# A gated recurrence interleaved with projection products: spawned twelve weight pieces earlier, at three steps to two pieces instead of four

## The chip, the cores and the metric

One core of a Trainium2 chip runs the whole program. The metric is the device time of one execution in microseconds (us); the table below gives the median of three executions of the kernel before.

## What is computed

The program is two transformer blocks on 256 tokens of width 1024, all in float32. The part that matters here lies near its start. The first block normalizes x, modulates it to h, and multiplies h by one wide matrix `w_in`, whose column groups feed several branches. One branch is a gated linear recurrence (`hgrn2`), eight heads of width 128:

```
f = lb + (1.0 - lb) * jax.nn.sigmoid(f_pre.astype(jnp.float32))
log_f = jnp.log(f)
kk = 1.0 - f
...
attn = jnp.einsum('bhtd,bhsd,bhtsd->bhts', qt, kt, decay)
o = (jnp.einsum('bhts,bhsv->bhtv', attn, vt)
     + jnp.einsum('bhtd,bhdv->bhtv', qt * jnp.exp(b), state))
```

Its inputs are the products bq (q), bf (f) and bi (v) of h with `w_in`. Other products of h (iq, ik, iw, aq, ak, av) feed a sparse attention, which comes after the recurrence in the program.

## The kernel before, in words

**Products by pieces.** Every product runs on TensorE as three fast passes (lines 579, 580, 581) over operands split into a high and a low part. Weights arrive by DMA from the SP queue into five slots, and are cut into pieces of 128x1024. For each piece ScalarE writes the high part (line 1398), VectorE the low part (line 2025), and TensorE then does 24 matmuls of 128x256 or 12 of 128x512. Four slots hold split pieces, so ScalarE and VectorE prepare piece n+3 while TensorE is at piece n; the high part of piece n+3 waits until piece n-1 has been used. When a piece ends a product, ScalarE copies the finished bank out (line 1420, or line 1426 with two copies), which waits for TensorE to end that very piece.

**The pieces in question**, in the order of the program behind the products bf and bq: bi (8 pieces), iq (4), ik (1), iw (1, with small matmuls of 128x8), aq (8), ak (8), av (8). This text numbers them 1 to 38: bi is 1 to 8, iq 9 to 12, ik 13, iw 14, aq 15 to 22, ak 23 to 30, av 31 to 38. Of aq and ak every second piece (16, 18, ... 30) ends a product; of av pieces 34 and 38.

**The recurrence by steps.** On each of the four engines `hgrn()` is a Python generator (TensorE line 709, ScalarE line 1466, VectorE line 2127, GpSimd line 2928) whose `yield`s cut it into 56 steps, 28 for each half of the heads. `Ticks` (line 69) runs it: after each piece `tick()` takes `rate` steps of the generator on that engine, and `join()` takes what is left. So the place of every instruction is set when the program is built, alike on all engines. In each half the steps are these: step 2 and 3 make two score tiles (line 720). Then come eight levels, and level l has its steps at 4+3l, 5+3l and 6+3l:

- step A (4+3l): ScalarE takes two exponentials (lines 1488 and 1494). VectorE multiplies Q (line 2150) and adds to P (line 2155). GpSimd multiplies K (line 2954) and adds to S (line 2957).
- steps T0 and T1 (5+3l and 6+3l): TensorE multiplies K and Q to a tile each (line 732, four matmuls of 128x128), and VectorE copies it by mask (line 2164).

A tile T0 waits for Q of VectorE and K of GpSimd of its level. Q waits for the first exponential and for T1 of the level before, K for the second exponential and for the same T1. Level 7 has one tile; behind it, steps 27 and 28 of a half form the outputs (lines 745, 747 and 748), the first of which waits for ScalarE to copy the tile of level 7 out (line 1501).

**Where it stands.** `ticks.spawn(hgrn(), 2)` stands behind bi and iq (TensorE line 1288). 26 pieces follow with 2 steps each, that is 52 steps; `ticks.join()` behind av takes the last four. The attention begins behind the join, and its first matmul (line 755) waits for two small loads, which the SP queue issues only after the last output of the recurrence (line 745 ff.) is done.

Of the kernel before, what the change touches and what calls it, by code (L numbers as in the profile page):

```python
# [70 lines left out]
class Ticks:  # L71
# [3 lines left out]
        self.gens, self.ended, self.all = [], set(), False  # L75

    def spawn(self, gen, rate=1):
        self.gens.append([gen, rate])

    def tick(self):  # L80
        for b in list(self.gens):
            for _ in range(b[1]):
                if next(b[0], "end") == "end":
                    self.gens.remove(b)
                    break
# [47 lines left out]
def build(nc, a, out, scr):  # L133
    with ExitStack() as ctx:
# [242 lines left out]
        def skey(p, what):  # L377

            return (what, p.j)
# [174 lines left out]
        def tensor(e, w):  # L554
            ticks = Ticks()
# [37 lines left out]
            def gemm1(name, X, ready, at=None):  # L593

                o = {}
                for p in walk(name):
                    if at and (p.g, p.k) in at:
                        enter(*at[p.g, p.k])
                    w.wait_ge(*skey(p, "L"))
                    for i in range(p.m):  # L600
                        k = p.k + i
                        w.wait_ge(*ready(k))
                        for t in range(2):
                            if k == 0:
                                o[t] = take("m", name, p.g, t)
                            rows = slice(128 * t, 128 * t + 128)
                            ins = three(o[t][:, 0:p.width], (X[0][:, k, rows], X[1][:, k, rows]),
                                        parts(p, i * p.width, p.width), k == 0, p.end and i == p.m - 1)
                    used(ins, p, *([(name, p.g, t) for t in range(2)] if p.end else []))
# [99 lines left out]
            def hgrn():  # L709
                for hf in range(2):  # L710
                    q_, k_ = bq[:, 1024 * hf:1024 * hf + 1024], bk[:, 1024 * hf:1024 * hf + 1024]
                    S_, Q_, K_, E_ = hg
                    yield
                    for tile in range(2):
                        w.wait_ge("kk")
                        w.wait_ge("bq", 3)
                        b = take("s", "hgd", hf, tile)
                        for g in range(4):
                            c = slice(256 * g + 128 * tile, 256 * g + 128 * tile + 128)
                            ins = e.matmul(b[:, 128 * g:128 * g + 128], k_[:, c], q_[:, c], start=True, stop=True)  # L720
                        full(ins, "hgd", hf, tile)
                        yield
                    for li in range(8):
                        yield
                        w.wait_ge("hgtQ", hf, li)
                        w.wait_ge("hgtK", hf, li)
                        for tile in range(2 if li < 7 else 1):
                            b = take("s", "hgl", hf, li, tile)
                            for g in range(4):
                                c = slice(256 * g + 128 * tile, 256 * g + 128 * tile + 128)  # L730
                                c2 = c if li < 7 else slice(256 * g + 128, 256 * g + 256)
                                ins = e.matmul(b[:, 128 * g:128 * g + 128], K_[:, c], Q_[:, c2], start=True, stop=True)  # L732
                            full(ins, "hgl", hf, li, tile)
                            yield
                    w.wait_ge("taken", ("hgl", hf, 6, 1))
                    w.wait_ge("taken", ("hgl", hf, 7, 0))
                    for t in range(2):
                        w.wait_ge("bi", 1)
                        b = take("s", "hgo", hf, t)
                        for g in range(4):  # L740
                            h = 4 * hf + g
                            o = b[:, 128 * g:128 * g + 128]
                            v = [bi[:, i * 1024 + h * 128:i * 1024 + h * 128 + 128] for i in range(2)]
                            if t == 0:
                                ins = e.matmul(o, hgA[:, g, 0:128], v[0], start=True, stop=True)
                            else:
                                e.matmul(o, hgA[:, g, 256:384], v[0], start=True, stop=False)
                                ins = e.matmul(o, hgA[:, g, 128:256], v[1], start=False, stop=True)
                        full(ins, "hgo", hf, t)
                        yield  # L750
# [511 lines left out]
            b = take("m", "c")  # L1262
# [8 lines left out]
            b = take("m", "rows", 0)  # L1271
# [8 lines left out]
            b = take("m", "rows", 1)  # L1280
            e.transpose(b[:, 0:128], vv0, K(C_ID))
            full(e.transpose(b[:, 128:145], vv3[0:17, :], K(C_ID)[0:17, 0:17]), "rows", 1)
            first()
            turn["m"] = 2
            gemm1("bi", hT, h_ready)
            gemm2("iq", hT, h_ready)
            w.wait_ge("consts")
            ticks.spawn(hgrn(), 2)
            for p in walk("ik"):
                w.wait_ge(*skey(p, "L"))  # L1290
                b = take("m", "ik")
# [3 lines left out]
            for p in walk("iw"):  # L1295
                w.wait_ge(*skey(p, "L"))
                for t in range(2):
                    b = take("m", "iw", t)
# [38 lines left out]
            for q in range(2):  # L1337
                b = take("s", "ws", q)
# [9 lines left out]
            for p in walk("kk"):  # L1348
# [3 lines left out]
                b = take("m", "kk2", p.g)  # L1352
# [17 lines left out]
        def scalar(e, w):  # L1370
            ticks = Ticks()
# [36 lines left out]
            def run(name, ev=None):  # L1408
                for p in walk(name):
                    if p.end and ev:  # L1410
                        ev(p)

            def copier(dst, ntot=None, scale=None, key=None):

                kw = {} if scale is None else {"scale": scale}

                def ev(p):
                    if ntot is None:
                        b = got(p.name, p.g)
                        taken(e.activation(dst[:, 512 * p.g:512 * p.g + 512], b[:, :], ACT.Copy, **kw), p.name, p.g,  # L1420
                              also=[(p.name, p.g)])
                    else:
                        for t in range(2):
                            b = got(p.name, p.g, t)
                            o = t * ntot + p.g * p.width
                            taken(e.activation(dst[:, o:o + p.width], b[:, 0:p.width], ACT.Copy), p.name, p.g, t,
                                  also=[(p.name, p.g, t), (p.name, t)])
                return ev
# [367 lines left out]
            b = got("c")  # L1796
# [43 lines left out]
            inc(e.activation(lb, lbz, ACT.Exp), "lb", ("lb1",))  # L1840
            ev_bq = copier(bq)
            run("first", lambda p: (ev_bf if p.name == "bf" else ev_bq)(p))
            run("bi", copier(bi, 1024))
            run("iq", copier(iq))
            w.wait_ge("consts")
            ticks.spawn(hgrn(), 2)

            for p in walk("ik"):
                b = got("ik")
                taken(e.activation(ik, b[:, 0:256], ACT.Copy), "ik", also=[("ik",)])  # L1850
            for p in walk("iw"):
                for t in range(2):
                    b = got("iw", t)
# [136 lines left out]
        def vector(e, w):  # L1990
            ticks = Ticks()
# [60 lines left out]
            def run(name, ev=None):  # L2052
                for p in walk(name):
                    if p.end and ev:
                        ev(p)
# [59 lines left out]
            def ev_bf(p):  # L2115
                g = p.g
                f, k_ = bf[:, 512 * g:512 * g + 512], bk[:, 512 * g:512 * g + 512]
                w.wait_ge("taken", ("bf", g))
                w.wait_ge("lb")
                for q in range(2):  # L2120
                    c, o = 2 * g + q, slice(256 * q, 256 * q + 256)
                    inc(e.tensor_scalar(f[:, o], f[:, o], omlb[:, c:c + 1], lb[:, c:c + 1], ALU.mult, ALU.add), "gate",
                        ("f", g, q))
                w.wait_ge("f", g, 1)
                inc(e.tensor_scalar(k_, f, -1.0, 1.0, ALU.mult, ALU.add), "gate", ("kk",))
# [609 lines left out]
            b = got("rows", 0)  # L2735
# [12 lines left out]
            b = got("rows", 1)  # L2748
# [17 lines left out]
            then(e.tensor_tensor(lb, lbz, lbz, ALU.subtract))  # L2766
            inc(e.tensor_scalar(omlb, lb, -1.0, 1.0, ALU.mult, ALU.add), "lb", ("lb",))
            run("first", lambda p: ev_bf(p) if p.name == "bf" else None)
            run("bi")
            run("iq")  # L2770
            w.wait_ge("consts")
            ticks.spawn(hgrn(), 2)
            run("ik")
            run("iw")
            run("aq")
# [138 lines left out]
        def gpsimd(e, w):  # L2914
            ticks = Ticks()
# [4 lines left out]
            def run(name, ev=None):  # L2920
                for p in G[name]:
                    if p.end and ev:
                        ev(p)
                    if p.end:
                        ticks.ended.add(p.name)
                    ticks.tick()
# [105 lines left out]
            inc(e.memset(eps[:, 1:2], LN_EPS), "eps", ("eps",))  # L3032
            w.wait_ge("consts")
            w.wait_ge("h", 3)
            run("bi")
            run("iq")
            ticks.spawn(hgrn(), 2)
            run("ik")
            run("iw")
            run("aq")  # L3040
# [234 lines left out]
```

## Time and profile before

| what | value |
|---|---|
| median of 3 runs | 2203.39 us (2203.15 to 2207.58) |
| the profiled execution | 2203.48 us |
| its span | 2201.6 us |
| TensorE matmul busy | 1992.5 us, 91% of the span |
| VectorE busy | 1111.1 us, 50% |
| ScalarE busy | 861.2 us, 39% |
| GpSimd busy | 123.2 us, 6% |
| mean granted TensorE clock | 0.963 |

The span is what the profiler saw between the first and the last instruction; the execution's own time has 1.9 us around it. Busy shares are means over a long program with many stages. The granted clock is the share of full speed (1.00 is 2.4 GHz, 0.50 is 1.2 GHz).

### The profile page before, as it was taken

Reading aid. Unit: us, or ns where it says so; the run is one execution under the profiler, and the core shown is the slowest. Engines: PE = TensorE matmul, PEld = TensorE weight load, DVE = VectorE, ACT = ScalarE, POOL = GpSimd, SP = SyncE. Lnnn points to the kernel's source line nnn. Section 1 sums busy time; section 2 is a strip of 40 time slices with the busy share of each in tenths; the row PEclk is TensorE's granted clock in tenths of the full one; section 3 lists DMA queues with packets and bytes.
Section 4 is the critical chain, followed back from the end, with each engine's and each line's share of the span. In section 5 each row is a group of like instructions: output and inputs, shape, how many; then the busy total and the mean of one; then the engine's idle time right before and its main releaser. Section 6 shows DMA issues by size and latency. Waiting matters only on the chain.

```text
span 2201.6 us, 30516 instructions
## 1 busy us (share of the span) xinstructions
PE 1992.5 (91%) x12952; PEld 1619.2 (74%) x12952; DVE 1111.1 (50%) x1418; ACT 861.2 (39%) x1131; POOL 123.2 (6%) x110
## 2 busy tenths in 40 slices
PE   8988899999999766676789999999999999969998
PEld 8988688889997211111148997888998999858997
DVE  6455495567764111011126555655556555675554
ACT  5444345554443100000024445545445444645443
POOL 0023212000210000000000000000000000020000
PEclk9999899999999998988899999999999999989999
DMA  9633344567888999999994655545554655305652
GB/s 375 202 97 98 96 139 148 172 197 248 290 316 324 391 424 423 423 424 423 422 386 162 231 191 159 185 157 169 191 191 137 209 185 183 131 20 173 199 174 76
DMA packets 242015, 503.17 MB, mean 229 GB/s; under 512 B 9681, under 2 KB 158514, under 8 KB 217426
## 3 DMA queue, kind: packets, MB, share of 16 engines
q1 hardware_dynamic: 241200, 500.27, 62.9%
q8 instruction: 104, 1.70, 0.3%
q10 hardware_dynamic: 530, 0.73, 0.1%
q0 software_dynamic: 144, 0.17, 0.1%
q14 instruction: 37, 0.30, 0.0%
HBM read 500.07 MB, written 1.06 MB: 228 GB/s over the span
## 4 chain that ended last, share of the span: by engine, by line
PE 72%; DMA 16%; DVE 6%; ACT 2%; issue 2%; POOL 1%; SPq 1%; DVEq 0%; POOLq 0%; ACTq 0%
PE bank L579 21%; PE bank L580 20%; PE bank L581 20%; DMA m<-in_expert_w_up 7%; DMA m<-in_expert_w_down 7%; PE bank L977 2%; PE bank L988 2%; DVE m L2025 1%; PE bank L732 1%; DMA m<-in_ffn_w_in 1%; PE bank L864 1%; DVE m L2678 0%; DMA m<-in_ada_w 0%; PE bank L636 0%; ACT m L1398 0%
## 5 line engine op out<-in xcount | busy, mean ns | idle before, releaser
L579 PE MATMUL bank<-m,m 128*128 128x256 f32 (+2 forms) x3240 | 1025.4, 316 | 20.0 <-DVE m L2025 6.9
L580 PE MATMUL bank<-m,m 128*128 128x256 f32 (+2 forms) x3240 | 1010.4, 312 | 0.0
L581 PE MATMUL bank<-m,m 128*128 128x256 f32 (+2 forms) x3240 | 1009.4, 312 | 0.0
L2025 DVE TENSOR_TENSOR m<-m,m 128x1024 fp32r<-128x1024 f32 x508 | 623.1, 1233 | 404.1 <-ACT m L1398 403.4
L1398 ACT ACTIVATE m<-m 128x1024 fp32r<-128x1024 f32 x508 | 531.4, 1056 | 383.3 <-PE bank L581 357.1
L579 PEld LDWEIGHTS bank<-m,m 128*128 128x128 f32 x3240 | 615.2, 190 | 66.4 <-issue 15.2
L580 PEld LDWEIGHTS bank<-m,m 128*128 128x128 f32 x3240 | 614.8, 190 | 37.6 <-issue 2.4
L581 PEld LDWEIGHTS bank<-m,m 128*128 128x128 f32 x3240 | 614.6, 190 | 36.9
L977 PE MATMUL bank<-m,m 128*32 128x512 f32 x1024 | 188.0, 683 | 67.3 <-DMA m<-in_expert_w_up 46.9
L977 PEld LDWEIGHTS bank<-m,m 128*32 128x32 f32 x1024 | 41.7, 122 | 205.0 <-DMA m<-in_expert_w_up 88.3
L988 PE MATMUL bank<-m,m 128*32 128x512 f32 x512 | 97.0, 721 | 34.1 <-DMA m<-in_expert_w_down 27.9
L988 PEld LDWEIGHTS bank<-m,m 128*32 128x32 f32 x512 | 22.0, 126 | 100.1 <-DMA m<-in_expert_w_down 55.1
L2452 DVE SCALAR_TENSOR_TENSOR m<-bank,m,m 128x512 f32<-128x512 f32 x8 | 6.0, 750 | 172.5 <-PE bank L977 172.5
L2458 DVE TENSOR_TENSOR m<-bank,m 128x512 f32<-128x512 f32 x16 | 10.3, 687 | 148.6 <-PE bank L988 148.6
L3023 POOL TENSOR_TENSOR m<-m,m 128x384 f32<-128x384 f32 x8 | 10.6, 1340 | 1290.5 <-DVE m L2674 1290.5
L1705 ACT ACTIVATE m<-m 128x512 f32<-128x512 f32 x44 | 27.8, 632 | 107.7 <-DVE m L2569 107.7
L1711 ACT ACTIVATE m<-m 128x512 fp32r<-128x512 f32 x44 | 27.8, 632 | 103.4 <-DVE m L2577 103.4
L1646 ACT ACTIVATE m<-bank 128x512 f32<-128x512 f32 x8 | 4.8, 597 | 151.3 <-PE bank L1038 151.3
L2040 DVE SCALAR_TENSOR_TENSOR m<-m,m,m 128x512 f32<-128x512 f32 x73 | 54.8, 751 | 6.5 <-DMA m<-in_ada_w 4.3
L1627 ACT ACTIVATE m<-m 128x512 fp32r<-128x512 f32 x16 | 9.4, 635 | 123.0 <-DVE m L2458 123.0
L732 PE MATMUL bank<-m,m 128*128 128x128 f32 x240 | 33.3, 290 | 19.7 <-issue 10.4
L2477 DVE TENSOR_TENSOR m<-m,bank 128x512 f32<-128x512 f32 x32 | 21.3, 686 | 54.4 <-PE bank L1059 54.4
(353 smaller groups left out, 1349.7 us busy)
## 6 DMA issues: line engine op xcount, KB each, us to landing
m<-in_ffn_w_in SPq DMA_DIRECT2D x88, 1024.0 KB, 5.1
m<-in_expert_w_gate SPq DMA_DIRECT2D x64, 1024.0 KB, 24.4
m<-in_expert_w_up SPq DMA_DIRECT2D x64, 1024.0 KB, 23.6
m<-in_w_in SPq DMA_DIRECT2D x63, 1024.0 KB, 5.1
m<-in_expert_w_down SPq DMA_DIRECT2D x60, 1024.0 KB, 25.4
m<-in_ffn_w_out SPq DMA_DIRECT2D x44, 1024.0 KB, 4.9
m<-in_ada_w SPq DMA_DIRECT2D x24, 1024.0 KB, 5.5
m<-in_a_w_in SPq DMA_DIRECT2D x16, 1024.0 KB, 5.2
```

What stands on the lines that cost most here:

```text
L579: e.matmul(o, s[0], m[0], start=first, stop=False, skip_group_check=skip)
L580: e.matmul(o, s[0], m[1], start=False, stop=False, skip_group_check=skip)
L581: return e.matmul(o, s[1], m[0], start=False, stop=last, skip_group_check=skip)
L732: ins = e.matmul(b[:, 128 * g:128 * g + 128], K_[:, c], Q_[:, c2], start=True, stop=True)
L864: ins = e.matmul(o[k // per][:, k % per * n:k % per * n + n], xs[part][:, i, 128 * k:128 * k + 128], rv(Sx[:, i, 128 * q0:128 * q1]), star ...
L977: ins = e.matmul(b[32 * j:32 * j + 32, :], XG[:, q, k, 32 * j:32 * j + 32], ld.raw[:, 512 * i:512 * i + 512], start=k == 0, stop=k == 7, s ...
L988: ins = e.matmul(b[n][32 * j:32 * j + 32, :], eT[q % 2][:, 128 * c + 32 * j:128 * c + 32 * j + 32], ld.raw[:, 1024 * i + 512 * n:1024 * i ...
L1398: inc(e.activation(rv(fit(q.H, q.view.shape)), q.view, ACT.Copy), "h", skey(q, "H"))
L1705: inc(e.activation(fb[4], fb[4], ACT.Silu), "ffn", ("fs", n, c))
L1711: inc(e.activation(fb[2 * (c % 2)].rearrange("p c n -> p (c n)"), fb[5], ACT.Copy), "ffn", ("fH", n, c))
L2025: inc(e.tensor_tensor(rv(fit(q.L, q.view.shape)), q.view, fit(q.H, q.view.shape), ALU.subtract), "l", skey(q, "L"))
L2040: ins = e.scalar_tensor_tensor(out=acc[g], in0=p.view[:, k, :], scalar=cs[:, 4 * q + k:4 * q + k + 1], in1=acc[g], op0=ALU.mult, op1=ALU.add)
```

## The change

The recurrence is spawned before the product bi and not behind iq, on all four engines. The rate becomes 1.5, and `Ticks` carries the half step over: the pieces take 1, 2, 1, 2, ... steps in turn. After 38 pieces 57 calls have been made, so `join()` finds nothing left.

```
@@ -75,11 +75,13 @@
     def spawn(self, gen, rate=1):
-        self.gens.append([gen, rate])
+        self.gens.append([gen, rate, 0])
 
     def tick(self):
         for b in list(self.gens):
-            for _ in range(b[1]):
+            b[2] += b[1]
+            while b[2] >= 1:
+                b[2] -= 1
                 if next(b[0], "end") == "end":
                     self.gens.remove(b)
                     break
@@ -1282,10 +1284,10 @@
             turn["m"] = 2
+            w.wait_ge("consts")
+            ticks.spawn(hgrn(), 1.5)
             gemm1("bi", hT, h_ready)
             gemm2("iq", hT, h_ready)
-            w.wait_ge("consts")
-            ticks.spawn(hgrn(), 2)
...
```

The same two lines move in the same way in the bodies of ScalarE and VectorE. GpSimd waited for the constants ahead of bi already; there only the spawn moves.

Place 1: ScalarE's program in the second half of the heads, while ak's pieces run. L1398 (L1400 in the changed file, where lines behind `Ticks` are two higher) is the high part of a piece, L1420 (L1422) the copy of a finished bank, L1488 and L1494 (L1490 and L1496) the two exponentials of a level. Before, levels 0 to 3 of the second half stand here:

```order
117 L1488 ACTIVATE m_130<-m_119 128x512
118 L1494 ACTIVATE m_130<-m_127 128x512
119 L1398 ACTIVATE m_57<-m_52 128x1024
120 L1398 ACTIVATE m_54<-m_53 128x1024
121 L1420 ACTIVATE m_133<-bank 128x512
122 L1488 ACTIVATE m_130<-m_119 128x512
123 L1494 ACTIVATE m_130<-m_127 128x512
124 L1398 ACTIVATE m_55<-m_53 128x1024
125 L1488 ACTIVATE m_130<-m_119 128x512
126 L1494 ACTIVATE m_130<-m_127 128x512
127 L1398 ACTIVATE m_56<-m_49 128x1024
128 L1398 ACTIVATE m_57<-m_49 128x1024
```

In the changed kernel, levels 1 to 3 of the same half:

```order
113 L1422 ACTIVATE m_133<-bank 128x512
114 L1490 ACTIVATE m_130<-m_119 128x512
115 L1496 ACTIVATE m_130<-m_127 128x512
116 L1400 ACTIVATE m_57<-m_50 128x1024
117 L1400 ACTIVATE m_54<-m_51 128x1024
118 L1422 ACTIVATE m_133<-bank 128x512
119 L1490 ACTIVATE m_130<-m_119 128x512
120 L1496 ACTIVATE m_130<-m_127 128x512
121 L1400 ACTIVATE m_55<-m_51 128x1024
122 L1400 ACTIVATE m_56<-m_52 128x1024
123 L1422 ACTIVATE m_133<-bank 128x512
124 L1490 ACTIVATE m_130<-m_119 128x512
```

Before, one pair of exponentials stood behind a copy out of a bank and the next pair stood free of one, in turn; now each pair of these levels stands right behind a copy.

Place 2: ScalarE's program in the first half of the heads, which now runs beside bi. In the changed kernel:

```order
60 L1400 ACTIVATE m_56<-m_50 128x1024
61 L1428 ACTIVATE m_122<-bank 128x512 x2
62 L1400 ACTIVATE m_57<-m_50 128x1024
63 L1490 ACTIVATE m_130<-m_119 128x512
64 L1496 ACTIVATE m_130<-m_127 128x512
65 L1400 ACTIVATE m_54<-m_51 128x1024
66 L1400 ACTIVATE m_55<-m_51 128x1024
67 L1490 ACTIVATE m_130<-m_119 128x512
68 L1496 ACTIVATE m_130<-m_127 128x512
```

Here each pair stands behind the high part of a piece that doesn't end a product, and the copies out (L1428 is L1426 of the file before) fall on the other pieces.

Place 3: TensorE's program at the end of av. Before, the last three tiles and both outputs (L745, and the eight rows that begin with L747 and L748) stand behind the last product of av:

```order
1179 L579 MATMUL bank<-m_55,m_117 128x512
1180 L580 MATMUL bank<-m_59,m_117 128x512
1181 L581 MATMUL bank<-m_55,m_118 128x512
1182 L732 MATMUL bank<-m_128,m_129 128x128 x12
1183 L745 MATMUL bank<-m_122,m_131 128x128 x4
1184 L747 MATMUL bank<-m_122,m_131 128x128
1185 L748 MATMUL bank<-m_122,m_131 128x128
```

In the changed kernel the first output (L747, the L745 of the file before) stands a piece earlier, behind piece 37, and only the second one behind piece 38:

```order
1169 L581 MATMUL bank<-m_54,m_117 128x512
1170 L582 MATMUL bank<-m_58,m_117 128x512
1171 L583 MATMUL bank<-m_54,m_118 128x512
1172 L747 MATMUL bank<-m_122,m_131 128x128 x4
1173 L581 MATMUL bank<-m_55,m_117 128x512
```

The tiles of levels 6 and 7 moved in front of pieces 35 to 37, and nothing but the second output is left behind av.

## Rows read from the trace of the kernel before

**Rows 1.** The page's busy times and shares, by engine.

```profile
PE 1992.5 (91%) x12952; PEld 1619.2 (74%) x12952; DVE 1111.1 (50%) x1418; ACT 861.2 (39%) x1131; POOL 123.2 (6%) x110
```

**Rows 2.** Stretches: length, TensorE busy (instructions), granted clock, DMA share, GB/s.

```profile
76.10:112.64 36.54, 36.54 (x219) 1.00 0.53 165
112.64:255.03 142.39, 121.97 (x851) 0.92 0.31 97
```

**Rows 3.** Timeline of TensorE: start, length in us, instruction, idle before and its releaser.

```profile
132.21 1.69 PE L732 MATMUL bank<-m,m 128*128 128x128 f32 x8 [3.21 <-issue]
148.17 1.16 PE L732 MATMUL bank<-m,m 128*128 128x128 f32 x8 [2.05 <-DVE m L2150]
165.16 1.13 PE L732 MATMUL bank<-m,m 128*128 128x128 f32 x8 [3.11 <-issue]
204.64 1.62 PE L732 MATMUL bank<-m,m 128*128 128x128 f32 x6 [3.22 <-issue]
219.97 1.16 PE L732 MATMUL bank<-m,m 128*128 128x128 f32 x8 [1.71 <-DVE m L2150]
234.44 1.59 PE L732 MATMUL bank<-m,m 128*128 128x128 f32 x8 [2.07 <-DVE m L2150]
247.75 1.28 PE L732 MATMUL bank<-m,m 128*128 128x128 f32 x8 [2.32 <-DVE m L2150]
249.76 2.05 PE L745 MATMUL bank<-m,m 128*128 128x128 f32 x8 [0.73 <-issue]
```

**Rows 4.** Stretches of the second of Rows 2, in the same columns.

```profile
118.80:124.20 5.40, 5.40 (x34) 0.68 0.00 0
132.20:137.60 5.40, 5.39 (x33) 0.68 0.08 10
148.20:153.50 5.30, 5.30 (x32) 0.68 0.49 182
165.20:170.40 5.20, 5.20 (x45) 1.00 0.12 17
204.60:209.80 5.20, 5.16 (x20) 0.70 0.03 3
234.40:239.80 5.40, 5.36 (x20) 0.68 0.22 57
247.70:255.00 7.30, 6.51 (x33) 0.57 0.01 2
```

**Rows 5.** Timeline of ScalarE, VectorE and GpSimd behind a piece that ends a product.

```profile
201.46 0.60 ACT L1420 ACTIVATE m<-bank 128x512 f32<-128x512 f32 x1 [4.48 <-PE bank L581]
202.50 0.67 ACT L1494 ACTIVATE m<-m 128x512 f32<-128x512 f32 x1
202.65 0.69 DVE L2150 TENSOR_TENSOR m<-m,m 128x512 f32<-128x512 f32 x1 [0.47 <-ACT m L1488]
203.25 1.29 POOL L2954 TENSOR_TENSOR m<-m,m 128x512 f32<-128x512 f32 x1 [5.30 <-ACT m L1494]
```

**Rows 6.** Timeline of TensorE: the first matmul of a piece and the tile behind it.

```profile
188.77 0.36 PE L579 MATMUL bank<-m,m 128*128 128x256 f32 x1
...
191.73 1.05 PE L720 MATMUL bank<-m,m 128*128 128x128 f32 x8
```

**Rows 7.** Timeline of ScalarE and TensorE at level 0 of the second half.

```profile
192.54 1.28 ACT L1488 ACT_TABLE_LOAD   x1
193.84 0.67 ACT L1488 ACTIVATE m<-m 128x512 f32<-128x512 f32 x1
...
196.56 2.02 PE L732 MATMUL bank<-m,m 128*128 128x128 f32 x16 [0.91 <-issue]
```

**Rows 8.** Timeline of ScalarE: two copies out where av ends a product.

```profile
223.97 1.09 ACT L1426 ACTIVATE m<-bank 128x512 f32<-128x512 f32 x2 [4.55 <-PE bank L581]
```

**Rows 9.** Timeline of VectorE: the Q product beside GpSimd's K product.

```profile
139.30 1.30 DVE L2150 TENSOR_TENSOR m<-m,m 128x512 f32<-128x512 f32 x1
```

**Rows 10.** Timeline of TensorE: the attention's first matmul behind the recurrence.

```profile
263.89 1.44 PE L755 MATMUL bank<-m,m 32*8 32x384 f32 x2 [5.65 <-DMA m<-in_buckets]
```

More of the change, by code:

```diff
@@ L77, in spawn @@
     def spawn(self, gen, rate=1):
-        self.gens.append([gen, rate])
+        self.gens.append([gen, rate, 0])
     def tick(self):
         for b in list(self.gens):
-            for _ in range(b[1]):
+            b[2] += b[1]
+            while b[2] >= 1:
+                b[2] -= 1
                 if next(b[0], "end") == "end":
@@ L1284, in tensor @@
             turn["m"] = 2
+            w.wait_ge("consts")
+            ticks.spawn(hgrn(), 1.5)
             gemm1("bi", hT, h_ready)
             gemm2("iq", hT, h_ready)
-            w.wait_ge("consts")
-            ticks.spawn(hgrn(), 2)
             for p in walk("ik"):
@@ L1842, in scalar @@
             run("first", lambda p: (ev_bf if p.name == "bf" else ev_bq)(p))
+            w.wait_ge("consts")
+            ticks.spawn(hgrn(), 1.5)
             run("bi", copier(bi, 1024))
             run("iq", copier(iq))
-            w.wait_ge("consts")
-            ticks.spawn(hgrn(), 2)
             for p in walk("ik"):
@@ L2768, in vector @@
             run("first", lambda p: ev_bf(p) if p.name == "bf" else None)
+            w.wait_ge("consts")
+            ticks.spawn(hgrn(), 1.5)
             run("bi")
             run("iq")
-            w.wait_ge("consts")
-            ticks.spawn(hgrn(), 2)
             run("ik")
@@ L3034, in gpsimd @@
             w.wait_ge("h", 3)
+            ticks.spawn(hgrn(), 1.5)
             run("bi")
             run("iq")
-            ticks.spawn(hgrn(), 2)
             run("ik")
```

## The prediction

> **What bounds the kernel now.** I read the page's busy times first: TensorE works in 91% of the span, every other engine in half of it or less [rows 1]. So a change of order can give back only what TensorE stands idle, or runs at a lower clock, in the stretch that it touches. Next the stretches by themselves. In the pieces of bi and iq and in ik (from 76.10 to 112.64), TensorE is busy all the time at full clock; from the first step of the recurrence to its end (112.64 to 255.03) it is busy for 121.97 of 142.39 us, at a mean clock of 0.92 [rows 2]. So 142.39 - 121.97 = 20.4 us are idle.
>
> The timeline of TensorE tells where: ten waits in front of tiles and outputs, eight of which stand in [rows 3]. The reader should look at two things. The three waits of 3.1 to 3.2 us fall where ScalarE's exponentials stand behind a copy that waits for the end of the very piece behind which the tile is wanted (releaser "issue": the last to come is GpSimd). The waits of 1.7 to 2.1 us are released by VectorE's Q product: two tiles were made together, and only one piece lies between them and the next tile.
>
> The clock costs as well. A stretch of L us, busy at a mean clock of c, loses L x (1 - c) against full clock. By [rows 4] that is 1.73, 1.73, 1.70, 0, 1.56, 1.73 and 3.14 us, in all 11.6 us. The first of these follows the tiny matmuls of iw, the others follow waits: of the five waits of 2 to 3.2 us within the pieces, four were followed by a granted clock of 0.50 for a while (1.2 GHz, the means are over a longer stretch), and one (165.16) was not. The last is the end of the recurrence, where 2.32 and 0.73 us of waiting are followed by both outputs at the lower level.
>
> So the stretch holds 20.4 + 11.6 = 32.0 us that a better order could give back.
>
> **The change part by part.** TensorE's matmuls are the same in number and form; so are the instructions of the other engines and all DMAs. Only the places change, so the sum is one of waits and of clock.
>
> *First half of the heads (pieces 1 to 19).* With 1, 2, 1, 2, ... steps, step A of level l is taken at piece 3+2l, an odd one, and both tiles at piece 4+2l. Between the tiles of one level and those of the next lie two pieces, of 191.73 - 188.77 = 2.96 us each [rows 6], 5.9 us together. How much is needed? Where two tiles were followed by one piece, the next tile came 2.05 us late [rows 3] (at 148.17), so the need is 2.96 + 2.05 = 5.0 us: covered. Where the exponentials stood behind a copy, they do no longer: odd pieces end no product, but for ik (13), behind which iw lies (5.4 us of small matmuls), more than the 3.2 us needed. So all of the eight levels run without a wait, also beside bi and iq, where nothing has stood idle so far. Moving the constants' wait on three engines I price at nothing: GpSimd has the same wait ahead of bi already, and a late one would show as idle time ahead of piece 1. One wait is new in this half: tile 7 and the first output now stand behind the same piece (18), and the output needs ScalarE's copy of that tile; it stood so at the end of the second half, for 0.73 us [rows 3] (at 249.76). Sum of this half: 0.7 us.
>
> *Second half (pieces 20 to 38).* Step 32, the first step A of this half, is an even number, and this turns the phase. Step A of level l and its first tile T0 now both fall to piece 22+2l, and T1 to piece 23+2l. Pieces 22, 24, 26, 28 and 30 end products of aq and ak, and there ScalarE's copy and then both exponentials come only after the end of the piece behind which T0 is wanted. That is the pattern of the 3.2 us wait, seen in full in [rows 5]: copy from 201.46, second exponential from 202.50, K product from 203.25 with 1.29 us, tile at 204.64.
> - Levels 1 to 4 pay it: 4 x 3.2 = 12.8 us.
> - Level 0 pays a table load on top. Before, a piece and a tile of the same step lay beside that chain; now nothing does. From the end of a piece (191.73, and 0.16 us until its last matmul ends) to the tile at 196.56 are 4.7 us [rows 6, 7].
> - Level 6 stands at piece 34, where two banks are copied out in 1.09 us and not one in 0.60 [rows 5, 8]: 3.2 + 0.5 = 3.7 us.
> - Levels 5 and 7 stand at pieces 32 and 36, which end nothing. Here the exponentials are early, and VectorE is the one to come last, with one piece as cover. The trace has no such place with one tile only: the bounds are nothing (all hidden) and the 2.07 us of two tiles in a row [rows 3] (at 234.44). I start from the nearest row, 1.71 us, take off one masked copy (0.7 us) and half a us by which VectorE was behind there: 0.5 us each, 1.0 us together.
>
> Sum of this half: 4.7 + 12.8 + 3.7 + 1.0 = 22.2 us.
>
> *The join.* No tile is left behind av. The waits of 2.32 and 0.73 us and 3.1 us of lower clock at the end go; they are in the sums of before. The last output stays behind the last piece of av, so the SP queue issues the attention's two small loads at the same point, and the wait of 5.65 us behind the first piece of cq stays as it is [rows 10].
>
> *The sum.* Idle: 0.7 + 22.2 = 22.9 us against 20.4, +2.5 us. Clock: the mean of the five waits within the pieces is (1.73 + 1.70 + 0 + 1.56 + 1.73) / 5 = 1.34 us. Six waits of over 3 us make 8.1 us, and iw keeps its 1.7: 9.8 us against 11.6, -1.8 us. Together +0.7 us on the profiled execution's 2203.5 us, which lies 0.1 us from the median of the runs: **2204.2 us**. What the first half wins (waits of 3.21, 2.05, 3.11 and 1.09 us), the second half loses, since every level meets a copy there.
>
> *Two rules of the Trainium skill.* VectorE's Q product took 1.30 us beside GpSimd's K product [rows 9] and 0.69 us where it started alone [rows 5]; at pieces 32 and 36 the two meet, and I counted the longer one. "SBUF — State Buffer", section "Who interferes with whom", says that a tensor_tensor with both inputs in SBUF and a GpSimd read exclude each other for a whole instruction. The trace agrees. Without that the 0.5 us would be hidden twice, and the sum would be 2203.2 us. ScalarE's table load took 1.28 us, and the exponential began 0.02 us behind it [rows 7]. "ScalarE: Activation LUTs", section "What ACT_TABLE_LOAD costs", adds a drain of about 1.38 us to each switch; the trace doesn't show it behind the load. By the page, level 0 would wait some 6.1 us, and the sum would be 2205.6 us.
>
> **The rivals.**
> - *The waits come, but the clock doesn't fall behind them.* For it speaks the wait of 3.11 us, behind which the clock stayed at 1.00 [rows 3, 4]; against it the other four. The sum loses 8.1 us: 2204.2 - 8.1 = 2196.1 us, faster. If half of them stay at full clock, the time is about 2200.
> - *The change does what its step count says in both halves:* two pieces of cover for every level, no wait but the 0.7 us. It would need the exponentials to be early in the second half too. Idle falls by 19.7 us and clock loss by 9.9: 2203.5 - 29.6 = 2173.9 us. The order of ScalarE's instructions, pair behind copy at every level, speaks against it.
> - *VectorE becomes the last at pieces 32 and 36 as well (slower).* Its place is the Q product of levels 5 and 7, behind the masked copy and the low part of a piece; its price decides from the point where Q ends more than 1.7 us behind the last matmul of the piece. Then these two wait 1.71 and 2.07 us, not 1.0 together: +2.8 us. And all eight waits are then long enough for the clock to fall, 1.7 us each: 8 x 1.7 + 1.7 = 15.3 us in place of 9.8, +5.5. That gives 2204.2 + 8.3 = 2212.5 us. For it speaks that four of five waits were followed by the lower clock and that VectorE was late by these amounts already; against it, that only one tile precedes now.
>
> **How the numbers follow.** A measurement of this kernel can tell about 0.2%, 4.4 us, from no change. The forecast of about no change gets 0.60: it holds with three to six of the six waits followed by the lower clock. The rival without clock loss gets 0.18, the full gain 0.04, VectorE's rival 0.18. Faster is then 0.22, the same 0.60, slower 0.18. The range begins at the first rival's 2196.1 and ends at 2210, short of the slower rival's full price; outside it are the full gain and the end of the slower case.
>
> **What would show it right or wrong.** In the changed profile, TensorE should have no idle time between piece 1 and tile 7 of the first half. Then should come waits in front of the tiles of line 734: about 4.7 us, four of 3.2, one of 3.7, with two near 0.5 us around the latter, each behind an end of a product, and idle near 23 us in all from the first piece of bi to the first of cq. The last output should come right behind av. I am wrong if the waits of the second half are missing, if waits show in front of tiles beside bi, or if the wait ahead of the attention grows, which would mean that the loads behind the recurrence got into the way of something else.

## The result, and the profile after

The changed kernel takes 2212.93 us (median of 14 executions, 2207.41 to 2219.21), the kernel before 2206.59 us beside it (14 executions, 2203.15 to 2211.19). The ratio is 1.0029, with a 95% interval of 1.0018 to 1.0041: slower by 0.29%, or 6.3 us. The forecast was +0.7 us, and the range ended at 2210. The three executions of before that were shown ahead of the prediction had a median of 2203.39 us; with 35 executions, at the end of the study, it stood at 2205.7 us. Of the 8.7 us between forecast and measurement, about 3 us are that base, and 5.6 us are mine.

The changed kernel scatters over 12 us, and its first profile is of its slowest execution (2219.21 us). I took a second profile of each kernel, and read the clock from both. First the page of the changed kernel, busy times:

```profile
span 2217.4 us, 30515 instructions
PE 2006.9 (91%) x12952; PEld 1635.4 (74%) x12952; DVE 1116.2 (50%) x1418; ACT 860.3 (39%) x1131; POOL 122.4 (6%) x110
```

ScalarE and GpSimd are as busy as before [rows 1] to within 1 us, VectorE is busy for 5.1 us more. TensorE is busy for 14.4 us more with the same number of matmuls: its mean granted clock over the whole program is 0.958, and was 0.963.

From TensorE's first matmul of bi to its first of cq, in each kernel's first profile (stretch, length, TensorE busy, granted clock, DMA share, GB/s). The kernel before:

```profile
76.10:254.88 178.78, 158.36 (x1067) 0.93 0.35 111
```

The changed kernel:

```profile
77.44:268.82 191.38, 168.11 (x1067) 0.88 0.33 104
```

The idle time is 178.78 - 158.36 = 20.4 us before and 191.38 - 168.11 = 23.3 us after, +2.9 us. The busy time is 9.8 us longer at a mean clock of 0.88 in place of 0.93. These two make 12.6 us of the 15.8 us between the two spans; of the rest, 1.3 us lie ahead of bi, and about 1.9 us behind this stretch.

The waits answer to [rows 3]. The timeline of TensorE, with its idle time before each instruction:

```profile
151.64 1.13 PE L747 MATMUL bank<-m,m 128*128 128x128 f32 x8 [0.73 <-issue]
172.49 2.05 PE L734 MATMUL bank<-m,m 128*128 128x128 f32 x8 [4.66 <-issue]
186.26 2.04 PE L734 MATMUL bank<-m,m 128*128 128x128 f32 x8 [3.23 <-issue]
199.82 2.05 PE L734 MATMUL bank<-m,m 128*128 128x128 f32 x8 [3.12 <-issue]
213.41 2.05 PE L734 MATMUL bank<-m,m 128*128 128x128 f32 x8 [3.10 <-issue]
227.05 2.05 PE L734 MATMUL bank<-m,m 128*128 128x128 f32 x8 [3.12 <-issue]
238.37 1.16 PE L734 MATMUL bank<-m,m 128*128 128x128 f32 x8 [0.87 <-DVE m L2152]
249.62 0.57 PE L734 MATMUL bank<-m,m 128*128 128x128 f32 x3 [3.60 <-issue]
259.64 1.16 PE L734 MATMUL bank<-m,m 128*128 128x128 f32 x8 [0.85 <-DVE m L2152]
277.74 1.44 PE L757 MATMUL bank<-m,m 32*8 32x384 f32 x2 [5.79 <-DMA m<-in_buckets]
```

The releaser "issue" means that the profile puts the wait down to no engine; who came last is seen in the next timelines. There is no wait beside bi and iq, none in the first half of the heads but the 0.73 us in front of its output, and then the row that was forecast: 4.7, four of 3.1 to 3.2, and 3.6 us, with two of 0.9 around the latter. The sum is 23.3 us (forecast 22.9). The wait of the attention is 5.79 us, against 5.65 [rows 10].

Why these waits stand there is seen at the second of them, in the timelines of ScalarE, VectorE and GpSimd:

```profile
183.06 0.60 ACT L1422 ACTIVATE m<-bank 128x512 f32<-128x512 f32 x1 [2.65 <-PE bank L583]
183.56 0.65 ACT L1490 ACTIVATE m<-m 128x512 f32<-128x512 f32 x1
184.11 0.68 ACT L1496 ACTIVATE m<-m 128x512 f32<-128x512 f32 x1
184.24 0.69 DVE L2152 TENSOR_TENSOR m<-m,m 128x512 f32<-128x512 f32 x1 [2.20 <-ACT m L1490]
184.87 1.29 POOL L2956 TENSOR_TENSOR m<-m,m 128x512 f32<-128x512 f32 x1 [11.01 <-ACT m L1496]
```

It is the pattern of [rows 5], line by line: copy out of the bank, two exponentials, GpSimd's K product (over at 186.16), tile (at 186.26). At level 0 the table load stands in between:

```profile
168.49 1.28 ACT L1490 ACT_TABLE_LOAD   x1
169.78 0.66 ACT L1490 ACTIVATE m<-m 128x512 f32<-128x512 f32 x1
```

The exponential begins 0.01 us behind the load, and the wait is 4.66 us, as the sum had it; the other price that the prediction gives for this level, some 6.1 us, did not come.

What is not as forecast is the clock. Three stretches of the changed kernel around that wait: the wait until the clock falls, the low level, and what follows.

```profile
183.00:185.40 2.40, 0.03 (x1) 1.00 0.00 0
185.40:192.20 6.80, 5.94 (x28) 0.50 0.13 22
192.20:196.70 4.50, 4.50 (x38) 0.99 0.52 200
```

The granted clock goes to 0.50 (1.2 GHz) while TensorE is still waiting, and stays there for 6.8 us. In the kernel before the low level held for 3.4 us at a wait of the same length (3.22 us, over at 204.64), though there too it began ahead of the wait's end:

```profile
204.20:207.60 3.40, 2.96 (x11) 0.51 0.02 5
```

The low levels at the other four of the first five long waits (level 0's with its 4.66 us among them) look the same:

```profile
171.80:178.60 6.80, 6.11 (x28) 0.50 0.15 31
199.10:205.90 6.80, 6.08 (x28) 0.50 0.15 34
212.80:219.60 6.80, 6.19 (x29) 0.50 0.16 36
226.40:233.20 6.80, 6.15 (x19) 0.50 0.16 36
```

From a late tile (one with such a wait in front) to the next tile there are 3.8 us at full clock (a tile and a piece). After 172.49, 186.26, 199.82, 213.41 and 227.05 the next tile starts 6.6 us later each time, after 249.62 it is 5.3 us. That is a loss of about 2.8 us five times and of 1.5 us once, 15.5 us in all; the forecast had 6 x 1.34 = 8.1 us. And the stretch from iw's first matmul on cost more than in the first profile of the kernel before:

```profile
124.70:142.40 17.70, 17.70 (x115) 0.71 0.35 108
```

Its loss is 17.70 x 0.29 = 5.1 us, where the forecast carried 1.7 us over from [rows 4]. The second profile of the kernel before, taken later, shows that this is not the change's doing. There too the clock fell inside iw, with no wait ahead of it, and stayed low for 10.2 us, again 5.1 us of loss:

```profile
118.20:128.40 10.20, 10.20 (x49) 0.50 0.09 30
```

In the second profile of the changed kernel it was low there for 3.4 us, as in [rows 4]:

```profile
128.80:132.20 3.40, 3.40 (x17) 0.50 0.01 2
```

So each kernel has shown both values, and 3.4 of the 9.8 us of busy time between the two first profiles are this scatter.

### The profile page after: what moved, and what is told of

Same layout as the page of the kernel before. It is cut to its first block, busy times and chain, and to the rows that moved or that the text cites. A ratio compares the mean times of both kernels' runs of the same rounds, so it can differ in the third digit from the quotient of the medians.

```text
span 2217.4 us, 30515 instructions
## 1 busy us (share of the span) xinstructions
PE 2006.9 (91%) x12952; PEld 1635.4 (74%) x12952; DVE 1116.2 (50%) x1418; ACT 860.3 (39%) x1131; POOL 122.4 (6%) x110
## 4 chain that ended last, share of the span: by engine, by line
PE 75%; DMA 16%; DVE 5%; ACT 2%; issue 1%; SPq 0%; DVEq 0%; POOL 0%; ACTq 0%
PE bank L581 21%; PE bank L583 21%; PE bank L582 21%; DMA m<-in_expert_w_up 8%; DMA m<-in_expert_w_gate 7%; PE bank L979 4%; PE bank L734 2%; DVE m L2027 1%; DMA m<-in_ffn_w_in 1%; PE bank L866 1%; DVE m L2680 0%; DMA m<-in_ada_w 0%; PE bank L638 0%; PE bank L679 0%; PE bank L667 0%
## 5 line engine op out<-in xcount | busy, mean ns | idle before, releaser
L1400 ACT ACTIVATE m<-m 128x1024 fp32r<-128x1024 f32 x508 | 531.6, 1056 | 418.3 <-PE bank L583 392.0
L581 PEld LDWEIGHTS bank<-m,m 128*128 128x128 f32 x3240 | 621.5, 192 | 66.0 <-issue 15.2
L582 PEld LDWEIGHTS bank<-m,m 128*128 128x128 f32 x3240 | 621.9, 192 | 37.7 <-issue 2.4
L583 PEld LDWEIGHTS bank<-m,m 128*128 128x128 f32 x3240 | 620.6, 192 | 37.3
L734 PE MATMUL bank<-m,m 128*128 128x128 f32 x240 | 37.8, 315 | 22.5 <-issue 20.8
L734 PEld LDWEIGHTS bank<-m,m 128*128 128x128 f32 x240 | 35.0, 225 | 25.2 <-issue 22.1
```

Source lines behind the costliest of these rows:

```text
L581: e.matmul(o, s[0], m[0], start=first, stop=False, skip_group_check=skip)
L582: e.matmul(o, s[0], m[1], start=False, stop=False, skip_group_check=skip)
L583: return e.matmul(o, s[1], m[0], start=False, stop=last, skip_group_check=skip)
L1400: inc(e.activation(rv(fit(q.H, q.view.shape)), q.view, ACT.Copy), "h", skey(q, "H"))
```

## The experiments

Theory A is the prediction's mechanism, with a larger price of the clock: the phase of the steps in the second half makes the waits, and the lower clock behind them makes the rest. Theory B: beginning sooner is what costs. Theory C: the waits alone count, not the clock. All shares of time below are read from TensorE's stretch from bi to cq.

### One empty step between the halves

```
                 for hf in range(2):
+                    if hf:
+                        yield
```

(in `hgrn()` of all four engines)

> The changed kernel with one empty step between the two halves of the heads on all engines, so that in the second half a level's exponentials and its first tile stand behind different pieces. Theory A (the waits and the lower clock behind them in the second half make the loss): TensorE's idle time from the first piece of bi to cq falls from 23.3 us to 1 to 4 us, the clock is low only behind iw, and the time is 20 to 38 us below the changed kernel, 2175 to 2193 us. Theory B (what costs is the first half's work beside bi and iq, and the lower clock behind iw): the second half's waits go, but the place near iw and something further on stays or grows, and the time stays within 8 us of the changed kernel.

Measured: 2178.07 us (4 executions, 2176.94 to 2179.11), ratio to the kernel before 0.9867 (0.9852 to 0.9883). Its waits from bi to the attention, and the stretch:

```profile
150.60 1.13 PE L749 MATMUL bank<-m,m 128*128 128x128 f32 x8 [0.73 <-issue]
170.49 1.13 PE L736 MATMUL bank<-m,m 128*128 128x128 f32 x8 [0.91 <-issue]
237.67 1.44 PE L759 MATMUL bank<-m,m 32*8 32x384 f32 x2 [5.59 <-DMA m<-in_buckets]
```

```profile
77.84:228.98 151.14, 149.50 (x1066) 0.98 0.42 131
```

With the first tile of a level moved one piece behind its exponentials, 23.3 us of idle time become 1.6 us, and TensorE's busy time falls from 168.1 to 149.5 us. The start beside bi and the rate are those of the changed kernel. Theory A holds and B falls: the early start and the rate cost nothing, and together they pay as soon as the phase is right. This version beats both kernels: it is 29.9 us below the 2207.96 us that the kernel before had beside it (18 executions), and 27.6 us below the 2205.7 us of all its 35.

### The exponentials ahead of the copy

```
+                    if early[0]:
+                        ticks.tick()
+                        yield p
+                        if p.end:
+                            ticks.ended.add(p.name)
+                        continue
```

(ScalarE's `walk`; `early[0]` is true from aq to av, and the caller copies the bank out after the `yield`)

> The changed kernel, but from aq to av ScalarE takes the recurrence's step ahead of the copy out of a finished bank, not behind it. Theory A (the exponentials behind the copy are what the tiles wait for): the five waits of 3.1 to 3.6 us shrink to VectorE's 0.9 us each, the one of level 0 to 1 to 2 us, idle is 7 to 9 us in place of 23.3, no low clock follows them, and the time is 2185 to 2198 us. Theory B: idle shrinks little, since VectorE or GpSimd comes last at nearly the same moment, and the time is 2208 to 2213 us.

Measured: 2186.87 us (5 executions, 2182.75 to 2189.01), ratio 0.991 (0.9896 to 0.9924). Two of its eight late tiles in the second half, then VectorE's Q product and GpSimd's K product ahead of the second one:

```profile
164.79 1.13 PE L734 MATMUL bank<-m,m 128*128 128x128 f32 x8 [1.43 <-issue]
181.85 1.16 PE L734 MATMUL bank<-m,m 128*128 128x128 f32 x8 [0.78 <-DVE m L2162]
```

```profile
180.03 1.76 DVE L2162 TENSOR_TENSOR m<-m,m 128x512 f32<-128x512 f32 x1
179.60 1.64 POOL L2966 TENSOR_TENSOR m<-m,m 128x512 f32<-128x512 f32 x1 [4.95 <-ACT m L1504]
```

The long waits shrink to 0.8 us, now released by VectorE, and level 0 waits 1.43 us. Idle is 7.9 us, and no low clock follows the waits of this size. So it was the copy ahead of the exponentials that the tiles waited for. The Q product took 1.76 us beside GpSimd here and not the 0.69 us that it takes alone: it ended 0.55 us after the K product had. That is what the tiles wait for next.

### The waits filled with useless matmuls

```
+                        first_b = None
+                        if hf and li < 7 and li != 5:
+                            first_b = take("s", "hgl", hf, li, 0)
+                            for _ in range(20 if li == 0 else 14):
+                                e.matmul(first_b[:, 0:128], K(C_ID), K(C_ONE), start=True, stop=True)
...
```

(`take` reserves the bank of the level's first tile; the useless products go into it, and the tile, which starts its sum afresh, overwrites them. A further line gives `first_b` to the first tile.)

> The changed kernel with useless matmuls of 128x128 in each of the six long waits of the second half (20 in front of level 0, 14 in front of levels 1 to 4 and 6, some 0.2 us each), into the bank that the tile takes next. Nothing is done sooner; only the clock can gain. Theory A (half of the loss is the lower clock behind evenly spaced waits): idle time is replaced by these matmuls, the clock stays at full behind them, and the time falls by 8 to 16 us, to 2197 to 2205 us. Theory C (the loss is the waits by themselves): the time stays at 2211 to 2216 us.

Measured: 2199.75 us (7 executions, 2198.07 to 2202.17), ratio to the kernel before 0.9971 (0.996 to 0.9982), 13.2 us below the changed kernel (12.8 us by the two ratios). No tile is wanted later or ready sooner than in the changed kernel: the second one below starts 3.3 us behind the end of its piece, against 3.2 us without the filling. The gain comes from work that nobody reads. The filled waits in the second half (the first one, and one of level 1):

```profile
169.59 0.68 PE L739 MATMUL bank<-m,m 128*128 128x128 f32 x4 [0.26 <-POOL m L2961]
180.60 1.13 PE L739 MATMUL bank<-m,m 128*128 128x128 f32 x8 [0.17 <-POOL m L2961]
```

In this profile the clock is low nowhere in the stretch but at iw. Theory C falls, and this is the clock's price by itself: 13.2 us, or 2.2 us for each of the six waits, and not the 1.34 of the prediction. The intervals of the two ratios leave about 3.5 us to either side of the 13.2, so the price lies between 1.6 and 2.8 us (an estimate).

### Half of each wait filled

The same edit with 14 and 7 matmuls in place of 20 and 14.

> The changed kernel with 14 useless matmuls in front of level 0 and 7 in front of levels 1 to 4 and 6, so that about 1.6 us of each of the five waits and 2 us of the first stay idle. If only waits of more than some 2 us lower the clock, the time is as with all of the wait filled, 2198 to 2202 us; if the clock falls by the length of the wait, half of the gain is lost, 2204 to 2208 us; if the waits alone count, 2211 to 2215 us.

Measured: 2203.58 us (12 executions, 2196.62 to 2206.47), ratio 0.999 (0.9982 to 0.9999). The median lies between the first two cases and decides for neither; that the waits alone count is excluded. The profile is of the fastest execution; there the waits left over are 1.6 to 2.1 us, and the clock fell behind none of them. The other executions take up to 10 us more, and their mean granted clocks are 0.961 to 0.968 against its 0.970, so in them the clock was low for longer somewhere in the program. Whether that was behind these waits no profile shows.

### Only the earlier start, and only the rate

The earlier start at the old rate: `ticks.spawn(hgrn(), 2)` at the new place.

> Only one part of the change: the recurrence begins twelve pieces sooner, at the old four steps to two pieces, so it ends at piece 28. Theory A: the waits of the kernel before come back in their old pattern (3.2, 2, 3.1, 1.1 us in each half, 15 to 20 us in all), no join is left, and the time is 2200 to 2207 us, a few us below both kernels. Theory B (an earlier start is what costs): the time is as the changed kernel's, 2211 to 2216 us.

Measured: 2210.55 us (12 executions, 2207.48 to 2212.57), ratio 1.0014 (1.0005 to 1.0024). A miss for theory A, by 3.5 us, and only 0.5 us short of theory B's 2211 to 2216, so this run by itself speaks for neither; the empty step does. The idle time is 21.8 us, where 15 to 20 us were expected. The second half has the waits that were expected, to within 0.1 us (3.22, 2.04, 3.12 and 1.10 us, with 0.91 us at level 0 ahead of them); the first half has more: 3.71, 1.70, 3.10 and 2.90 us, the last two of which are these.

```profile
125.60 2.05 PE L734 MATMUL bank<-m,m 128*128 128x128 f32 x8 [3.10 <-issue]
142.21 2.05 PE L734 MATMUL bank<-m,m 128*128 128x128 f32 x8 [2.90 <-issue]
```

The second of them now fell right in front of iw, and the clock fell as it ended. All of iw's tiny matmuls then ran at the low level, 10.24 us from its first matmul to the next tile, at full clock 5.4 us; in all the level held for 17.1 us, a loss of 8.5 us where iw costs 1.7 to 5.1 us in the profiles of the two kernels:

```profile
143.91:154.15 10.24, 10.24 (x51) 0.50 0.01 2
142.20:159.30 17.10, 17.09 (x81) 0.50 0.08 27
```

So the miss is this loss and the idle time in excess of the expected 20 us, as far as one profile can tell.

The rate of three steps to two pieces at the old place (`ticks.spawn(hgrn(), 1.5)` behind iq, with the new `Ticks`):

> The other part of the change by itself: three steps to two pieces, but begun at the old place, so that 39 steps are taken in the pieces and the last 17 in the join behind av. Theory A: levels 3 to 7 of the second half run with no product beside them, each with some 2 to 4 us of waiting, and at low clock; the time is 2215 to 2225 us, slower than both kernels. Theory B (the rate is what helps and the early start is what costs): at or below the kernel before, 2200 to 2207 us.

Measured: 2209.48 us (10 executions, 2208.21 to 2213.44), ratio 1.0018 (1.0009 to 1.0027). Slower than the kernel before, as theory A says, but less than it says. In the join each of the five levels left waits 2.0 us for VectorE's Q, the lower end of the 2 to 4 us expected, and TensorE is at the low level for much of the time in between. Two of these waits, and the stretch from the first of them to cq:

```profile
231.57 2.84 PE L734 MATMUL bank<-m,m 128*128 128x128 f32 x16 [2.00 <-DVE m L2152]
252.25 1.31 PE L734 MATMUL bank<-m,m 128*128 128x128 f32 x8 [2.00 <-DVE m L2152]
```

```profile
231.57:259.40 27.83, 19.07 (x96) 0.64 0.00 1
```

The first half has no wait but the 0.73 us at its output; in the second, waits of 5.12, 0.86 and 3.60 us stand ahead of the join. So neither part alone is a gain. Both together are a gain when the exponentials come out from behind the copy, by the empty step or by ScalarE's other order; neither part was run alone with that.

### Both kernels again

> The changed kernel itself, for a second profile: its executions spread over 12 us, and the first profile is the slowest of them. If the waits are fixed by the order and the clock behind them is what varies, the waits in front of the tiles are again within 0.2 us of 4.7, 3.2, 3.1, 3.1, 3.1, 0.9, 3.6 and 0.9 us, while the loss by the clock from the first piece of bi to cq is another than the 20.6 us of the first profile, less by as much as its time is shorter.

The profiled execution took 2210.95 us (median of 8: 2215.24; ratio to the kernel before 1.0042, 1.0028 to 1.0056). The waits in front of the tiles are those of the first profile to 0.1 us; three of them:

```profile
181.40 1.13 PE L734 MATMUL bank<-m,m 128*128 128x128 f32 x8 [3.21 <-issue]
192.22 1.13 PE L734 MATMUL bank<-m,m 128*128 128x128 f32 x8 [3.12 <-issue]
204.57 2.05 PE L734 MATMUL bank<-m,m 128*128 128x128 f32 x8 [3.11 <-issue]
```

Behind them the clock did three different things (stretch, length, busy, clock, DMA share, GB/s):

```profile
203.90:210.70 6.80, 6.13 (x29) 0.50 0.16 44
181.40:185.21 3.81, 3.81 (x33) 1.00 0.00 0
193.70:197.10 3.40, 3.40 (x19) 0.51 0.05 7
```

Behind the wait that ended at 181.40 it stayed at full; behind 192.22 it fell 1.4 us after the wait's end and held low for 3.4 us; at 204.57 it had fallen 0.7 us ahead of the wait's end and held low for 6.8 us. The stretch from bi to cq took 183.65 us, 7.7 us less than in the first profile, with the same 23.2 us of idle time: nearly all of the 8.3 us between these two executions.

> The kernel before itself, for a second profile. Its idle time from 112 to 255 us should be 20 to 21 us again; the loss by the clock may differ from 11.6 us by as much as the time differs.

The profiled execution took 2209.99 us (median of 8: 2204.27), the idle time in the stretch is 20.4 us again, and the busy time 160.7 us against 158.4. That is 2.3 of the 6.5 us between the two profiled executions of this kernel; the rest lies outside the stretch. Over both profiles of each kernel the stretch is 7.6 us longer after the change, 2.9 us of it idle and 4.7 us busy, and iw's loss is the same in both (1.7 and 5.1 us).

## Why the prediction was wrong

**The order and the waits were right.** The phase of the second half, the 4.7 us with the table load, the four waits of 3.2 us, the 3.7 us behind two copies, the cover of two pieces in the first half, and the unchanged wait of the attention came out as worked out, within 0.2 us each in the first profile. The two waits of VectorE at pieces 32 and 36 measured 0.87 and 0.85 us, forecast 0.5: +0.7 us together. Idle rose by 2.9 us, forecast 2.5.

**The step that failed is the term of the clock.** The prediction put it so: "the mean of the five waits within the pieces is (1.73 + 1.70 + 0 + 1.56 + 1.73) / 5 = 1.34 us", and took 8.1 us for six waits. In the two profiles of the changed kernel the twelve long waits cost 2.8, 2.8, 2.8, 2.8, 2.8, 1.5 and 2.3, 0, 1.5, 2.8, 2.8, 1.5 us (from a late tile to the next, less the time at full clock), a mean of 2.2, and filling them gave 13.2 / 6 = 2.2 us each. With 2.2 for 1.34 the sum is 0.7 + 6 x 0.86 = +5.9 us, against the 6.3 us measured. (Read from tile to tile, the prediction's five waits cost 1.2 us and not 1.34; like for like the sum is +6.7 us.) The loss of 6.3 us is thus about 2.9 us of waiting and, as what is left, 3.4 us of clock.

The five waits were not misread. The second profile of the kernel before has them again, four followed by 3.4 us of the low level and one by none, with the same mean. What failed is that their price was carried over to waits that stand otherwise: eight of the twelve in the changed kernel were followed by 6.8 us of it. [Rows 4] held one such level, the 7.30 us at 0.57 in the join, but it was left out of the mean. In the first profile the five levels of 6.8 us follow each other at 13.6 to 13.7 us, from 171.8 us on, and the late tiles at 13.6 to 13.8 us. So each of these waits met the clock as the one before it had, and the five are not five independent readings of a price. No run changed the distance of the waits, so this reason is read off, not shown.

**iw.** Its 1.7 us, carried over as it was, is one of two values that both kernels show; it was 5.1 us in one profile of each. It does not tell the change from the kernel before.

**The base.** The 2203.5 us on which the sum was put lay 2 to 3 us below the median of more executions (2206.6 us of 14, 2205.7 us of 35). That is no part of the mechanism, but it adds to the distance between forecast and measurement.

**The rivals.** That the clock would not fall was the wrong way round. The slower rival named VectorE at pieces 32 and 36 and a fall of the clock behind every wait. Its first half did not come (0.9 us each, not 1.7 to 2.1); its second half, that nearly every wait is followed by the low level, was what decided (11 of 12), and at a higher price than the 1.7 us it was given. That its 2212.5 us lies 0.4 us from the measured median is luck: 2.8 us of waiting and the fall behind two short waits, which did not come, stand in for the 3 us of the base and the higher price. The full gain, priced at -29.6 us and given 0.04, is what the empty step brought: 27.6 to 29.9 us, by the reference. The price was right to about 2 us, and so was the reason why this change would not have it.

**What stays open.** Why the low level holds 3.4 us after some waits and 6.8 us after others is only read off, not tested. The profiles of both kernels and of the early start at the old rate have 30 waits of 2 us and more ahead of tiles. Behind 4 the clock stayed at full. Eight had a low level that began 0.6 us or more ahead of the wait's end, and it held for 6.8 us. In the other 18 it began later, at most 0.5 us ahead of the end, and held for 3.4 us, but for two, which are followed by iw or by the small waits of the join. No run shifted a wait against the clock on purpose.

## What to carry to other kernels

When steps of one chain are dealt out between pieces of another, it isn't the mean density that counts but where each step falls in the pattern of the other chain: write down, for each level, which instruction stands ahead of it on every engine, in every half, as the parity may turn between two halves. Here one empty step turned a loss of 6 us into a gain of 28 to 30 us. And price a wait of TensorE of 2 us or more with the clock behind it: waits of 3.1 us cost about 5.3 us each here. A price read in one order of the waits did not hold in another, so take it from the new order, or fill the waits with matmuls and measure.

## What the runs showed of the hardware

- The lower clock behind a wait can last longer than the wait: 6.8 us at 1.2 GHz behind 3.1 us of idle time, in which TensorE was busy all the time but for the first 0.6 to 0.8 us. The same wait, in the same program, was followed by nothing, by 3.4 or by 6.8 us of it.
- The clock fell at small matmuls with no wait ahead of them. In nine of the ten profiles (the early start at the old rate is the tenth) TensorE had not waited between bi's first matmul and iw, and yet the clock fell 2.7 to 5.5 us after the first of its 48 matmuls of 128x8 and stayed low for 3.4 us (four profiles), 6.8 us (three) or 10.2 us (two, one of each kernel); the sooner it fell, the longer it held.
- Behind a wait it was worse: from the first of these matmuls to the next instruction it took 10.2 us, at the low level all along, where it had been 5.4 us at full clock.
- A VectorE product that met GpSimd's was done 0.55 us after it: 1.76 us in place of 0.69 us.
- Executions of one program scatter by 2.2 to 11.8 us, and not by their long waits alone: the kernel with the exponentials ahead of the copy, whose waits are 1.4 us and less, scatters by 6.3 us (five executions), the one with the empty step by 2.2 us (four). Of the 8.3 us between two executions of the changed kernel 7.7 us lay in the stretch from bi to cq, at equal idle time; of the 6.5 us between two of the kernel before, 2.3 us.
